# Eight attention heads in a two-block fp32 kernel: who scales the probabilities, where the modulation dots stand, and how the PSUM banks rotate behind them

## The reference

```python
# first block, once
h   = modulate(x, norm1_g, sh1, sc1)              # rmsnorm(x) * g * (1 + scale) + shift
q, k, v, gates, zh = split(h @ w_in + b_in)
y_hy = hyena(zh) @ w_hy_out
y_na = neighbourhood_attention(rope(q), rope(k), v, k_ctx, v_ctx, rpb) @ w_na_out
x  = x + g1 * ((sigmoid(g_hy) * y_hy + sigmoid(g_na) * y_na) @ w_out)
x  = x + g2 * peer(modulate(x, norm2_g, sh2, sc2))   # 8 heads, 16 experts each, rows gathered
# second block, twice (layers 0 and 1)
x  = x + hybrid_mixer(rms_norm(x))    # sparse attention and a state-space branch, both gated, @ w_out
x  = x + conv_glu_ffn(rms_norm(x))    # up projection, 3-tap convolution, silu gate, down projection
```

## Time and profile before

| | us |
|---|---|
| three runs of the kernel before | 2214.75, 2215.47, 2208.92 (median 2214.75) |
| the profiled execution's own time | 2212.09 |
| its span, first to last instruction | 2210.3 |

### The profile page before, as it was taken

The page is one execution under the profiler, slowest core; times in us unless marked ns, Lnnn a source line. Parts: engine busy times, 40 slices in busy tenths (PEclk is TensorE's granted clock), DMA queues, the critical chain, the costliest instruction groups (busy, mean ns, idle before and its releaser), DMA issues.

```text
span 2210.3 us, 27141 instructions
## 1 busy us (share of the span) xinstructions
PE 1984.0 (90%) x9640; PEld 1469.2 (66%) x9640; DVE 1377.4 (62%) x2782; ACT 1002.8 (45%) x1836; POOL 1048.6 (47%) x840
## 2 busy tenths in 40 slices
PE   7999968987877787777999999999999999998998
PEld 1777756943323333333599777889989977777998
DVE  3768955486666676665457754167763775326776
ACT  1623435332222212212445687455564567845555
POOL 2362657764444444443387757900028865692000
PEclk9999979999898989999999999999999999999999
DMA  9242765699999999999655444545555534454553
GB/s 350 68 138 82 253 222 174 211 421 421 422 422 421 421 421 422 421 422 421 229 178 172 136 162 159 173 157 187 187 156 189 181 124 155 160 180 163 191 182 114
DMA packets 111447, 534.40 MB, mean 242 GB/s; under 512 B 12496, under 2 KB 12880, under 8 KB 77904
## 3 DMA queue, kind: packets, MB, share of 16 engines
q1 hardware_dynamic: 67104, 244.72, 33.1%
q0 software_dynamic: 38720, 275.96, 30.4%
q10 hardware_dynamic: 5488, 11.98, 1.7%
HBM read 531.49 MB, written 1.11 MB: 241 GB/s over the span
## 4 chain that ended last, share of the span: by engine, by line
PE 59%; DMA 22%; DVE 6%; ACT 6%; issue 3%; POOL 3%; ACTq 0%; POOLq 0%; DVEq 0%; SPq 0%
PE psum L877 57%; DMA pair_rows<-in_peer_uv,arena 11%; DMA arena<-in_peer_uv,arena 6%; DMA wring<-in_peer_uv,arena 3%; PE psum L945 2%; ACT w_hi L1440 2%; POOL w_lo L2811 2%; POOL w_lo L2809 1%; ACT arena L1451 1%; ACT arena L1785 1%; DVE arena L2551 1%; DMA wring<-in_w_in_hy 1%; DMA wring<-in_w_ada 0%; ACT arena L1730 0%; DVE arena L2567 0%
## 5 line engine op out<-in xcount | busy, mean ns | idle before, releaser
L2809 POOL TENSOR_TENSOR w_lo<-wring,w_hi 128x512 fp32r<-128x512 f32 x280 | 382.4, 1366 | 543.8 <-ACT w_hi L1440 535.5
L1440 ACT ACTIVATE w_hi<-wring 128x1024 fp32r<-128x1024 f32 (+1 forms) x414 | 433.7, 1054 | 334.4 <-PE psum L877 313.0
L877 PE MATMUL psum<-w_hi,a_hi 128*128 128x512 f32 (+1 forms) x1056 | 425.1, 403 | 44.8 <-POOL w_lo L2811 15.2
L877 PE MATMUL psum<-w_lo,a_hi 128*128 128x512 f32 (+1 forms) x1056 | 412.9, 391 | 0.0
L877 PE MATMUL psum<-w_hi,a_lo 128*128 128x512 f32 (+1 forms) x1056 | 412.3, 390 | 0.0
L877 PE MATMUL psum<-arena 128*128 128x512 f32 (+7 forms) x1142 | 336.3, 451 | 65.2 <-ACT arena L1658 50.7
L2811 POOL TENSOR_TENSOR w_lo<-wring,w_hi 128x512 fp32r<-128x512 f32 x280 | 394.8, 1410 | 0.0
L877 PE MATMUL psum<-a_hi,w_hi 128*128 128x256 f32 x1312 | 376.7, 287 | 4.1 <-DVE a_lo L1930 2.3
L877 PE MATMUL psum<-a_hi,w_lo 128*128 128x256 f32 x1312 | 372.0, 284 | 0.0
L877 PE MATMUL psum<-a_lo,w_hi 128*128 128x256 f32 x1312 | 371.9, 283 | 0.0
L877 PEld LDWEIGHTS psum<-arena 128*128 128x128 f32 (+2 forms) x1142 | 186.0, 198 | 198.0 <-issue 126.6
(11 more groups left out here) (261 smaller groups left out, 2393.7 us busy)
## 6 DMA issues: line engine op xcount, KB each, us to landing
wring<-in_w_up SPq DMA_DIRECT2D x88, 512.0 KB, 3.3
wring<-in_w_xbc SPq DMA_DIRECT2D x48, 512.0 KB, 3.3
wring<-in_w_dn SPq DMA_DIRECT2D x44, 512.0 KB, 3.3
wring<-in_w_adaT SPq DMA_DIRECT2D x32, 512.0 KB, 4.3
wring<-in_w_qkv SPq DMA_DIRECT2D x32, 512.0 KB, 3.6
wring<-in_w_z SPq DMA_DIRECT2D x32, 512.0 KB, 3.2
wring<-in_w_g SPq DMA_DIRECT2D x32, 512.0 KB, 3.3
wring<-in_w_ps SPq DMA_DIRECT2D x32, 512.0 KB, 3.3
```

Source lines behind the costliest of these rows:

```text
L877: mm = lambda o, a, b, start, stop: nc.tensor.matmul(o, a, b, start=start, stop=stop, skip_group_check=True)
L1440: a.reaches(A(w_hi[:, n % SPLIT_RING, 0:width], wring[:, c % RING, 0:width], ACT.Copy), hi_ready, n + 1)
L2809: nc.gpsimd.tensor_tensor(w_lo[:, r, 0:half], wring[:, c % RING, 0:half], w_hi[:, r, 0:half].bitcast(F32), ALU.subtract)
```

## The change

- ScalarE scales the probabilities by the inverse sums (two instructions of 128 x 512 per head, behind the head's two exponentials) in place of VectorE, which now only makes the reciprocals and signals each.
- VectorE makes each head's three modulation dots at the end of its part of the head, behind `gate_bias` and `na_low` of the former head, no longer between the maxima and the reciprocals.
- The rotation of PSUM banks is set back to 2 by the gate tiles alone. Every rotating tile from mix(2) to the end has its bank moved by two.
- In the plan, the seventh chunk of `w_out` and of each layer's `w2_o` counts as used two turns later; ScalarE is told by hand to split the eighth one ahead of the first tile's read (`first_half`, `half_read`). In the second tile's softmax of layers 0 and 1, ScalarE splits the last two `w2_z` chunks ahead of the exponentials.
- `tiles_turned` opens each bank just ahead of its first transpose, in place of all eight at once.
- GpSimd's low part of `w_pq` chunk 1 waits for VectorE's first low part of the queries' input, in place of the last scaled tile.

```diff
@@ -248,7 +248,7 @@
         elif name in NA_BANKS:
             banks_ = NA_BANKS[name]
             b = banks_[i % len(banks_)]
-            r = 2
+            r = 2 if name == "gate" else r
         else:
             b, r = r, (r + 1) % BANKS
         bank[(name, i)], before[(name, i)] = b, held[b]
@@ -360,12 +360,16 @@
 
     w = []
 
-    def rows(name, out, n, groups, k_parts=4, l=None, first=0, split=True, width=CHUNK):
+    def rows(name, out, n, groups, k_parts=4, l=None, first=0, split=True, width=CHUNK,
+             last_by_tile=False):
 
         for j in range(n):
             a, b = groups(j)
             for k in range(k_parts):
                 ends = k == k_parts - 1
+                if last_by_tile and j == n - 1 and k == k_parts - 2:
+                    w.append((name, l, first + j * k_parts + k, width, turn[(out, b)] + 1, False, split))
+                    continue
                 w.append((name, l, first + j * k_parts + k, width, turn[(out, b)] + 1 if ends else turn[(out, a)],
                           ends, split))
 
@@ -386,7 +390,7 @@
     at = len(w)
     rows("w_hy_out", "mix", 2, two, 2)
     rows("w_na_out", "mix", 2, lambda j: (4 + 2 * j, 5 + 2 * j), 2)
-    rows("w_out", "wout", 2, two)
+    rows("w_out", "wout", 2, two, last_by_tile=True)
     for n in reversed(range(LATE_DOTS)):
         w.insert(at + LATE_AT[n], ("w_adaT", None, ADA_DOTS - LATE_DOTS + n, CHUNK, turn[LATE_AFTER[n]] + 1, True, False))
     for m in range(16):
@@ -400,7 +404,7 @@
         rows("w2_g", L + "gate", 4, two, l=l)
         rows("w2_pa", L + "pa", 2, two, l=l)
         rows("w2_ps", L + "ps", 2, two, 8, l=l)
-        rows("w2_o", L + "wo", 2, two, l=l)
+        rows("w2_o", L + "wo", 2, two, l=l, last_by_tile=True)
         for c in range(FT // 2 + 1):
             if c < FT // 2:
                 w.extend(("w2_up", l, 4 * c + m, CHUNK, turn[(L + "up", 4 * c + m)] + 1, True, True) for m in range(4))
@@ -949,9 +953,11 @@
 
         def tiles_turned(name, n):
 
-            o = [open_(name, k) for k in range(KD)]
+            o = []
             for t in range(TT):
                 for k in range(KD):
+                    if not t:
+                        o.append(open_(name, k))
                     if k % 4 == 0:
                         pe.wait_ge(S("tile_scaled"), 4 * n + 2 * t + k // 4 + 1)
                     m = nc.tensor.transpose(o[k][:, tile(t)], xs[:, t, tile(k)], ident)
@@ -1585,6 +1591,11 @@
                     read_out("nas", 2 * h + t, nap[h % 2][:, t, :], bank("nas", 2 * h + t), ACT.Exp,
                              bias=amax[:, 2 * h + t:2 * h + t + 1],
                              accum_out=asum[:, 2 * h + t:2 * h + t + 1])
+                for t in range(TT):
+                    i = 2 * h + t
+                    act.wait_ge(S("na_inverse"), i + 1)
+                    a.reaches(A(nap[h % 2][:, t, :], nap[h % 2][:, t, :], ACT.Copy, scale=ainv[:, i:i + 1]),
+                             S("na_prob"), i + 1)
             if h == 0:
                 act.wait_ge(S("c_row_in"), 16)
                 a.reaches(A(dve_junk[:], dve_junk[:], ACT.Silu), S("c_row_ready"), 1)
@@ -1604,6 +1615,8 @@
         for n in range(2):
             read_out("gb", n, G[:, 0, 512 * n:512 * n + 512], bank("gb", n))
         def first_half(i):
+            if i == 0:
+                weights_upto(act, "w_out", None, 7)
             due(act, "wout", i)
             wait_read(act, "wout", i)
 
@@ -1724,6 +1737,8 @@
             def exponentials(t, first):
                 n_keys = P * (t + 1)
                 act.wait_ge(S("max2"), TT * l + t + 1)
+                if t:
+                    weights_upto(act, "w2_z", l, first + 1)
                 for h in range(H2):
                     if h in (2, 5):
                         weights_upto(act, "w2_z", l, first + (h == 5))
@@ -1823,7 +1838,12 @@
                     weights_upto(act, *(("w2_o", l, 4) if k else ("w2_ps", l, 14)))
                 read_high(L + "mT", k, a_hi[:, k, :], bank(L + "mT", k)[:, 0:SEQ])
 
-            norm_tiles(1 + 2 * l, range(4), lambda i: wait_read(act, L + "wo", i))
+            def half_read(i):
+                if i == 0:
+                    weights_upto(act, "w2_o", l, 7)
+                wait_read(act, L + "wo", i)
+
+            norm_tiles(1 + 2 * l, range(4), half_read)
             scaled_high(L + "fT", KD, f"ffnw{l}")
             def glu_high(c):
                 for m_ in range(2):
@@ -2260,19 +2280,15 @@
                          S("na_max"), i + 1)
             if 0 < h < NA_HEADS - 1:
                 masked_bias(h + 1)
-            if h:
-                ada_dots(DOTS_PER_HEAD * (h - 1), DOTS_PER_HEAD * h)
             for t in range(TT):
                 i = 2 * h + t
                 wait_read(dve, "nas", i)
-                v.done(T.reciprocal(ainv[:, i:i + 1], asum[:, i:i + 1]))
-                v.settle()
-                v.reaches(T.tensor_scalar(nap[h % 2][:, t, :], nap[h % 2][:, t, :], ainv[:, i:i + 1], None, ALU.mult),
-                         S("na_prob"), i + 1)
+                v.reaches(T.reciprocal(ainv[:, i:i + 1], asum[:, i:i + 1]), S("na_inverse"), i + 1)
             if h:
                 if h % 2 == 0:
                     gate_bias(h // 2 - 1)
                 na_low(h - 1)
+                ada_dots(DOTS_PER_HEAD * (h - 1), DOTS_PER_HEAD * h)
         early = ADA_DOTS - LATE_DOTS
         ada_dots(early - DOTS_PER_HEAD, early)
         gate_bias(NA_HEADS // 2 - 1)
@@ -2802,7 +2818,7 @@
             pool.wait_ge(hi_ready, n + 1)
             width, r = wplan[c][3], n % SPLIT_RING
             if c == chunk_at[("w_pq", None, 1)]:
-                pool.wait_ge(S("tile_scaled"), 4)
+                pool.wait_ge(S("modulated_lo"), 2 * KD + 1)
             if second_block + 2 <= c < second_block + SPLIT_RING:
                 pool.wait_ge(S("pair_used"), split_freed((SPLIT_RING + r) * CHUNK))
             half = width // 2
```

## The result

The kernel before ran 2211.84 us (median of 4 runs, 2205.25 to 2215.47), the changed one 2245.09 us (median of 4, 2244.91 to 2246.59): ratio 1.0164, 95% interval 1.0145 to 1.0182. It is slower by 1.64%, some 33 us; the forecast was 2221, its own range ended at 2230 and the one for 8 in 10 at 2233. The profiled execution took 2245.19 us, its span 2243.4. The side was right and the size was not.

The account below looks back on a forecast made before the run. The prediction took TensorE, busy 90%, to bound the kernel, with VectorE pacing the attention heads. Its terms, +15.3 +2.2 +3.9 -9.0 -0.2 -4.6 +1.0 = +8.6 us on 2212.1, gave 2221; own range 2214 to 2230, 8 in 10 2202 to 2233.

Parts of the forecast that it names:

- The loop: Attention: a closed chain from nao(h-1) to nao(h) makes heads 14.5 us instead of 11.95, +15.3 us over six.
- The lower level: Rival, attention: TensorE at the lower clock level in every head, 15.6 us each, +16.8 in all, 2229 us; chance 0.18.
- The ring: Weight ring slots freed by dots: late chunks counted for the last head, within its +3.9 us; no term for six others.
- Heads 0 and 1: Start of attention: four scalings of 0.54 us ahead of nao(0), +2.2 us, bounds 0 and +3.
- The last head: Last attention head: later dots free the `w_hy_out` slots later, so the first split is late; +3.9 us, bounds +2.3 and +5.5.
- The merge: Merge behind the heads: new banks remove TensorE's 13 us stall ahead of mix(2); -9.0 us, bounds -6 and -10.
- The smaller gain: Merge: GpSimd's chunks or the last dots' weights hold VectorE, -6 instead of -9, 2224 us; forecast with it, chance 0.34.
- The `hfT` edits: Stage `hfT`: an extra split costs +0.75 us, VectorE's first low part is shorter; -0.2 in all, bounds -1 and +1.
- The softmax: Second tile's softmax: TensorE's 2.12 us wait goes, VectorE's L2599 is next late and does not move; -4.6 us, both layers.
- Output projection and up(0): Layers' output projection up to up(0): earlier splits against up(0)'s wait for fT(6); +1.0 us for both layers.
- The rotation's term: Ahead of up(0): its bank now follows fT(6) instead of fT(0), +1.6 to +3.3 us per layer.
- The relief of VectorE: Rival, attention: less VectorE work lets heads fall to TensorE's 10.19 us, -17.3 us in all, 2195 us; chance 0.18.

Follow-up runs that it names:

- rotation_only: The kernel before with the PSUM bank rotation alone, set back at a gate tile only; 2212.82 us, ratio 1.0008.
- warm7: The changed kernel plus seven idle matmuls ahead of TensorE's wait for the reads of nap in heads 1 to 6; 2240.02 us (one run).
- between_up_mixed: The kernel of between_up with VectorE, not ScalarE, scaling the probabilities of heads 0 and 1; 2196.90 us, ratio 0.9938.
- dots_between: The changed kernel with each head's three dots behind the next head's reciprocals and ahead of gate biases and low part; 2205.55 us, ratio 0.9970.
- thin_dots: The changed kernel with the first eighteen modulation dots made over 128 columns instead of 1024; 2237.80 us (one run).
- warm: The changed kernel plus twelve idle matmuls ahead of TensorE's wait for the reads of nap in heads 1 to 6; 2241.11 us, ratio 1.0128.
- between_up: The kernel of dots_between with the feed-forward's up tiles in banks 2, 3, 0, 1 instead of 0, 1, 2, 3; 2196.63 us, ratio 0.9935.

## Why the prediction was right or wrong, step by step

- **The loop.** That a loop closes was right, and so were the first terms of the way it summed: to the end of the exponentials it had 4.13 + 3.42 = 7.55, measured 7.57 (263.52 to 271.09). The step that failed is "I take 14.5; bounds 13.7 and 15.6": the heads took 16.4 us, and six cost +26.5 us, not +15.3. Of the 16.5 us of the head above against the sum of 13.72: nao 3.75 instead of 1.97 (+1.8), the two splits with their waits for `w_in` chunks 2.6 from the scalings' end, where 1.90 stood (+0.7), scalings 1.33 instead of 1.08 (+0.25). The lower level stood there as a rival; the argument against it, a window at clock 1.00, says little, since that window ends at 261.50 with the wait of 2.46 us and the matmul behind it starts at 261.55. Here TensorE waits 3.4 to 6.0 us in every head. Of the signs that it named, the dots directly behind the low part and none near 2.28 us came true; the reads 13.7 to 15.6 us apart did not.
- **The ring.** The chunk that a dot frees was seen for the last head alone. It was put at nothing in the six others, where the chain of waits runs over it in every head. So the way that the prediction summed is not the one that sets the pace, and that its first terms fit the trace is no proof of it; the two ways differ by about a microsecond.
- **Heads 0 and 1.** +2.2 forecast; the kernels with ScalarE's scaling read nao(0) at 229.4 to 231.7, those without it, the trace of before left out, at 225.2 to 226.3: some +4.5. Against `rotation_only` the first reads of nap come 2.45 us later behind the first exponential, which is the scalings, and from there to nao(0)'s read it is 4.75 us instead of 3.19: nao(0) took 3.54 us at the lower level, which the term left out.
- **The last head.** +3.9 forecast, +4.7 measured (+6.3 against the 16.1 us that six of the other kernels show there). The queue's timeline and the DMA view of the changed kernel, to the earlier trace rows:

```profile
332.76 1.75 SPq L842 DMA_DIRECT2D wring<-in_w_hy_out  x4
```

```profile
wring<-in_w_hy_out SPq DMA_DIRECT2D x4, 512.0 KB, 5.8
```

The issue comes 4.35 us behind nao(6)'s read at 328.41 (4.3 forecast) and the first split 8.9 (8.8 forecast); the later chunks land in 5.8 us and not in 4.5, and hold the second and third split.
- **The merge.** -9.0 forecast, -7.1 measured, inside the bounds. The smaller gain was foreseen by its cause, the weight of the second dot behind mix(3), but it is 2.3 us late and not 1. GpSimd does not hold VectorE at mix(6), but it holds it through the ring. The chain of the changed kernel:

```profile
361.34 2.25 POOL w_lo L2827
363.61 0.33 SPq L842
363.98 5.39 DMA wring<-in_w_adaT
```

The dot's chunk stands in SP's queue behind a `w_out` chunk, and that one waited until GpSimd had made the low part of the chunk whose ring slot it takes.
- **The `hfT` edits.** -0.2 forecast. The first low part takes 0.41 us instead of 1.38, as forecast; the stage as a whole (+1.3) shows nothing that the kernels without these edits (+1.7, +1.9) do not.
- **The softmax.** -4.6 forecast, nothing measured. The step by which VectorE's L2599 is next late and does not move failed twice. TensorE's timeline of the changed kernel:

```profile
1294.66 5.35 PE L949 MATMUL psum<-consts,arena 128*128 128x128 f32 x32 [2.35 <-issue]
```

TensorE ends its tiles early, idles 2.35 us and does the 32 transposes in 5.35 us, where 3.65 was the time in the earlier trace rows (the granted clock is 0.53 in the first 2.34 us of them). And L2599 (now L2615) did move:

```profile
1292.27 2.29 DVE L2615 TENSOR_TENSOR arena<-arena,small_values 128x2048 f32<-128x2048 f32 x1
```

It starts 33.12 us later than in the earlier trace rows, while the stage as a whole stands 31.7 later. ScalarE now makes the split and then a function table load of 1.28 us between the maxima and the exponentials; before, it had loaded the table at 1245.80, ahead of its wait for the maxima.
- **Output projection and up(0).** +1.0 forecast for both layers, +3.8 measured (-7.1 + 10.9). The rotation's term was sized at +1.6 to +3.3 per layer and cost 3.0 and 3.9 alone; the edits gave 2.1 net.
- **The relief of VectorE.** A false rival for this order of work, and true for the order next to it.

The excess over the forecast is some 24.5 us: 11.2 from the loop, 5.3 from the softmax, 2.8 from the output projection, 1.9 from the merge, 1.8 from heads 0 and 1, 0.8 from the last head, and the rest from stages that the forecast left alone. The sum of the terms as measured, +4.0 +26.5 +4.7 -7.1 +0.7 +3.8 = +32.6 (for heads 0 and 1 the 6.3 of the table less the 2.3 of the start), stands against +33.1 between the two profiled executions; what is left (start +2.3, peer stage and its sides +1.3, group norm -3.0, small rests) nearly cancels. What stays open is the size of the clock's part in single stages: it shifts by 1 to 3 us between executions of kernels that do not differ there.

## What to carry to other kernels

Work that is moved between engines carries its waits with it: ask what stands behind it in the new engine's order, and follow that until it closes on itself. In a loop over heads, look for all closed ways, the one through the weight ring too, and put filler work where its engine waits for the loop's slow link, as the dots between reciprocals and low part: the same instructions in three orders took 10.5, 15.4 and 16.4 us per head. A wait taken away from TensorE can come back as a lower clock behind the next wait, so cost the matmuls behind every new idle stretch at both levels.

## What the hardware showed that was not expected

- TensorE's level in this loop followed its waits closely: idle 1.2 to 1.4 us ahead of nao kept 1.97 us for its eight matmuls (`warm7`), idle 2.0 to 2.6 us gave 1.97 in some heads (`warm7`, `between_up_mixed`), 2.47 in one (`dots_between`) and 3.09 to 3.75 in others (`thin_dots`, `warm`, `between_up`), idle 3.4 us and more in the changed kernel 3.40 to 3.75. Seven fillers that compute nothing were worth 1.2 to 1.6 us in the three heads where they left such a short wait, and 0.8 in the mean of six.
- A transfer of 512 KB to the ring took 3.6 us from issue to landing (median of 28, `w_in`) before and 4.2 in the changed kernel. In the six heads they took 3.5 to 4.9 us before, issued 1.1 us apart; in the changed kernel three transfers are issued 0.4 to 0.5 us apart behind the third dot, and the second, on which the chain runs, took 5.3 to 6.2.
- ScalarE's scaling of 128x512 in SBUF with a scale from a column takes 0.67 us (1.33 for two); VectorE's takes 0.49 alone and 1.29 beside GpSimd.
